# Stick-breaking attention of a two-block layer stack: its eight heads taken two at a time

## What is computed

```python
def stick_breaking(q, k, v):          # for each head and each block of 128 queries
    z = einsum("bhqd,bhkd->bhqk", qi, kh) * scale
    mask = kpos[None, :] < qpos[:, None]
    sp = where(mask, softplus(z), 0.0)
    rev = cumsum(sp, axis=3, reverse=True)
    w = exp(where(mask, z - rev, -inf))
    return einsum("bhqk,bhkd->bhqd", w, vh)
```

## Time and profile before

| what | us |
|---|---|
| median of three runs (lowest, highest) | 3726.54 (3718.42, 3730.17) |
| the profiled execution's own time | 3731.72 |
| its span, first to last instruction | 3729.7 |
| TensorE busy in it | 3562.5 (96%) |
| VectorE, ScalarE, GpSimd busy | 1577.5, 1385.2, 1464.3 |
| mean granted TensorE clock | 0.968 of full speed |

### The profile page before, as it was taken

The page is one execution under the profiler, slowest core; times in us unless marked ns, Lnnn a source line. Parts: engine busy times, 40 slices in busy tenths (PEclk is TensorE's granted clock), DMA queues, the critical chain, the costliest instruction groups (busy, mean ns, idle before and its releaser), DMA issues.

```text
span 3729.7 us, 39657 instructions
## 1 busy us (share of the span) xinstructions
PE 3562.5 (96%) x16304; PEld 2811.6 (75%) x16304; DVE 1577.5 (42%) x2130; ACT 1385.2 (37%) x2241; POOL 1464.3 (39%) x785
## 2 busy tenths in 40 slices
PE   7999999999999999999999999998989999989999
PEld 5887766777888788766787788775577787777887
DVE  4326563454432433755436343345535411443220
ACT  3444444223331444444323322254532323543221
POOL 2333333443554332333344455433034543224543
PEclk9999999999999999999999999988899999999999
DMA  6333211444553333311253555412025532212332
GB/s 208 106 103 114 62 46 51 124 141 124 166 171 109 103 113 101 110 51 44 72 144 113 152 164 151 126 54 62 0 65 162 164 94 87 70 53 85 96 96 74
DMA packets 566978, 385.30 MB, mean 103 GB/s; under 512 B 13598, under 2 KB 504302, under 8 KB 566798
## 3 DMA queue, kind: packets, MB, share of 16 engines
q1 hardware_dynamic: 564574, 379.56, 34.8%
q10 hardware_dynamic: 2224, 3.21, 0.3%
HBM read 379.25 MB, written 2.10 MB: 102 GB/s over the span
## 4 chain that ended last, share of the span: by engine, by line
PE 82%; DVE 7%; ACT 6%; POOL 3%; issue 1%; DMA 1%; SPq 0%; ACTq 0%; DVEq 0%; POOLq 0%
PE ps L174 81%; POOL wlo L144 2%; ACT whi L140 2%; ACT L136 1%; PE ps L178 1%; DVE H L152 1%; DVE mq L152 0%; ACT sxb L136 0%; DVE fg L152 0%; DVE ST L158 0%; DVE np L144 0%; DVE sp L152 0%; DMA W<-in_w_ada 0%; ACT xr L136 0%; ACT sp L136 0%
## 5 line engine op out<-in xcount | busy, mean ns | idle before, releaser
L144 POOL TENSOR_TENSOR wlo<-raw,whi 128x1024 fp32r<-128x1024 f32 (+1 forms) x540 | 1281.3, 2382 | 1944.4 <-ACT whi L140 1943.5
L174 PE MATMUL ps<-UH,whi 128*128 128x512 f32 x2656 | 1072.2, 404 | 26.8 <-ACT UH L140 16.2
L174 PE MATMUL ps<-UH,wlo 128*128 128x512 f32 x2656 | 1050.4, 395 | 26.2 <-POOL wlo L144 26.2
L174 PE MATMUL ps<-UL,whi 128*128 128x512 f32 x2656 | 1047.5, 394 | 0.0
L140 ACT ACTIVATE whi<-raw 128x1024 fp32r<-128x1024 f32 (+1 forms) x540 | 545.5, 1022 | 387.7 <-PE ps L174 193.5
L174 PEld LDWEIGHTS ps<-UH,whi 128*128 128x128 f32 x2656 | 507.0, 191 | 158.0 <-ACT UH L140 27.2
L174 PEld LDWEIGHTS ps<-UH,wlo 128*128 128x128 f32 x2656 | 507.3, 191 | 148.2 <-POOL wlo L144 38.3
L174 PEld LDWEIGHTS ps<-UL,whi 128*128 128x128 f32 x2656 | 506.1, 191 | 109.1 <-DVE UL L144 2.2
L152 DVE SCALAR_TENSOR_TENSOR ACC<-raw,SM,ACC 128x512 f32<-128x512 f32 x308 | 357.0, 1159 | 20.4 <-DVE GL L144 0.5
L174 PE MATMUL ps<-GH,whi 128*128 128x512 f32 x704 | 275.1, 391 | 0.0
L174 PE MATMUL ps<-GL,whi 128*128 128x512 f32 x704 | 274.0, 389 | 0.0
(11 more groups left out here) (335 smaller groups left out, 4260.7 us busy)
## 6 DMA issues: line engine op xcount, KB each, us to landing
raw<-in_w_in SPq DMA_DIRECT2D x168, 512.0 KB, 4.0
raw<-in_w SPq DMA_DIRECT2D x120, 512.0 KB, 5.1
raw<-in_ada_w SPq DMA_DIRECT2D x96, 512.0 KB, 4.8
raw<-in_w_ada SPq DMA_DIRECT2D x80, 512.0 KB, 4.8
raw<-in_ffn_w_gate SPq DMA_DIRECT2D x44, 512.0 KB, 3.9
raw<-in_ffn_w_up SPq DMA_DIRECT2D x44, 512.0 KB, 3.9
raw<-in_ffn_w_down SPq DMA_DIRECT2D x32, 512.0 KB, 4.0
raw<-in_ev_w_in SPq DMA_DIRECT2D x20, 512.0 KB, 3.8
```

What stands on the lines that cost most here:

```text
L144: return self.e.tensor_tensor(o, a, b, op).then_inc(*self.done(*keys))
L174: m = self.e.matmul(o, l, r, start=start, stop=stop)
```

## The change

Heads 2i and 2i + 1 are now handled as pair i on every engine. On TensorE the matmuls of the two alternate: in scores one reads rows 0 to 63 and the next rows 64 to 127, and in values one writes columns 0 to 63 of the array and the next columns 64 to 127. Scores of three pairs are issued before the first sums, and those of the fourth behind the sums of the first pair. Values of pair i stand behind the sums of pair i + 1, those of the last pair at the end. Score banks are 0 to 3 (were 0 to 2), sum banks 4 and 5 (were 3 to 5). There are eight `zs` tiles, the four new ones in the space of the normalised input, which has been consumed by then, and four `sp` tiles. ScalarE runs both Exp of a pair and then both Ln. The number of matmuls and their sizes stay the same, and so do VectorE's and GpSimd's.

```diff
-              zs=[at(f"zs{i}", (32, 37, 42, 72)[i], [128, 1280]) for i in range(4)],
-              sp=[at(f"sp{i}", 77 + 5 * i, [128, 1280]) for i in range(3)])
+              zs=[at(f"zs{i}", (32, 37, 42, 72)[i], [128, 1280]) for i in range(4)] +
+                 [at(f"zs{4 + i}", 68 + 5 * i, [128, 1280], F32, BASE) for i in range(4)],
+              sp=[at(f"sp{i}", 77 + 5 * i, [128, 1280]) for i in range(3)] + [at("sp3", 89, [128, 1280], F32, BASE)])
...
+                for x in range(2):
+                    h, r = 2 * i + x, slice(64 * x, 64 * x + 64)
+                    o = bank(p, (0, 1, 2, 3), ("z", h, kb), ("dve", ("z", h, kb)))
+                    p.mm(o[:, 0:n], EV["QK"][r, 4 + i, kb * 128:(kb + 1) * 128], EV["QK"][r, i, kb * 128:512],
+                         True, True, ("z", h, kb))
...
-                o = bank(p, (3, 4, 5), ("su", h, kb), ("dve", ("su", h, kb)))
+                o = bank(p, (4, 5), ("su", h, kb), ("dve", ("su", h, kb)))
...
+                for x in range(2):
+                    h = 2 * i + x
+                    p.wait_ge(*on("act", "ew", h, kb))
+                    p.mm(pv[64 * x:64 * x + 64, 128 * kb:512], EV["V"][:, kb, h * 64:(h + 1) * 64],
+                         EV["zs"][h][:, OFF[kb]:OFF[kb + 1]], kb == 0, kb == 3, *([("epv", i)] if kb + x == 4 else []))
+
+        scores(0)
+        scores(1)
+        scores(2)
+        for i in range(4):
+            later_keys(2 * i)
+            later_keys(2 * i + 1)
+            if i == 0:
+                scores(3)
+            else:
+                values(i - 1)
+        values(3)
...
+        for i in range(4):
+            weights(i)
+            if i < 2:
+                soft(i + 2)
+            if i:
+                out_tile(i - 1)
+        out_tile(3)
...
+        scores(0)
+        softs(0)
+        scores(1)
+        softs(1)
+        sums(0)
+        scores(2)
+        sums(1)
+        for i in range(4):
+            less(2 * i)
+            if i < 3:
+                sums(2 * i + 2)
+            less(2 * i + 1)
+            if i < 3:
+                sums(2 * i + 3)
+            if i == 0:
+                scores(3)
+            if i < 2:
+                softs(i + 2)
+            if i:
+                out_tile(i - 1)
+        out_tile(3)
```

More of the change, by code:

```diff
@@ L2255, in pe_even, with scores @@
                 lambda b: (v_lane(b), ("EV", b)), UH, UL, None, between)
-        def scores(h):
-            i, po = h // 2, 64 * (h % 2)
-            if h == 0:
+        def scores(i):
+            if i == 0:
                 for w in range(2):
@@ L2264, in scores, with later_keys @@
                 n = 512 - 128 * kb
[L2265 to L2273, removed]
+                for x in range(2):
[3 more added lines that the diff above has]
+                         True, True, ("z", h, kb))
+        def later_keys(h):
+            sp = EV["sp"][h % 4]
             p.wait_ge(*on("dve", "sp", h))
@@ L2280, in pe_even, with values @@
                          *([("su", h, kb)] if k2 == 3 else []))
-            if h < 6:
-                scores(h + 2)
-            if h == 0:
+        def values(i):
+            if i == 0:
                 for b in range(4):
                     p.wait_ge(*on(v_lane(b), "EV", b))
-            if h % 2 == 0:
-                pv = bank(p, (6, 7), ("epv", i), ("dve", ("eyl", 4 + i)))
+            pv = bank(p, (6, 7), ("epv", i), ("dve", ("eyl", 4 + i)))
             for kb in range(4):
-                p.wait_ge(*on("act", "ew", h, kb))
-                p.mm(pv[po:po + 64, 128 * kb:512], EV["V"][:, kb, h * 64:(h + 1) * 64], z[:, OFF[kb]:OFF[kb + 1]],
-                     kb == 0, kb == 3, *([("epv", h)] if kb == 3 else []))
+                for x in range(2):
[9 more added lines that the diff above has]
+            later_keys(2 * i + 1)
+            if i == 0:
+                scores(3)
+            else:
+                values(i - 1)
+        values(3)
     def xy(k):
@@ L2367, in act_even, with soft, weights, out_tile @@
         copy_ev(a)
[L2369 to L2374, removed]
+        def soft(i):
+            for x in range(2):
+                h = 2 * i + x
+                a.wait_ge(*on("dve", "ab", h))
+                a.af(EV["sp"][h % 4][:, :], EV["sp"][h % 4][:, :], ACT.Exp, ("ex", h))
+            for x in range(2):
+                h = 2 * i + x
+                a.wait_ge(*on("act", "ex", h))
+                a.af(EV["sp"][h % 4][:, :], EV["sp"][h % 4][:, :], ACT.Ln, ("ln", h), bias=1.0)
+        def weights(i):
+            for x in range(2):
+                h = 2 * i + x
+                for kb in range(4):
+                    z = EV["zs"][h][:, OFF[kb]:OFF[kb + 1]]
+                    a.wait_ge(*on("dve", "su", h, kb))
+                    a.af(z, z, ACT.Exp, ("ew", h, kb))
+        def out_tile(i):
+            a.wait_ge(*on("pe", "epv", i))
+            a.cp(EV["YH"][:, 4 + i, :], ps(("epv", i))[:, :], ("eyh", 4 + i))
         soft(0)
         soft(1)
[L2378 to L2388, removed]
+        for i in range(4):
[5 more added lines that the diff above has]
+        out_tile(3)
     def copy_ev(e):
@@ L2444, in dve_even, with scores, softs, sums @@
         copy_ev(v)
-        def scores(h):
-            z, sp = EV["zs"][h % 4], EV["sp"][h % 3]
+        def scores(i):
             for kb in range(4):
                 n = 512 - 128 * kb
-                if h > 3:
[L2451 to L2460, removed]
+                for x in range(2):
+                    h = 2 * i + x
+                    v.wait_ge(*on("pe", "z", h, kb))
+                    v.cp(EV["zs"][h][:, OFF[kb]:OFF[kb] + n], ps(("z", h, kb))[:, 0:n], ("z", h, kb))
+        def softs(i):
+            for x in range(2):
+                h = 2 * i + x
+                z = EV["zs"][h]
+                v.wait_ge(*on("pool", "zm", h))
+                if h > 3:
+                    v.wait_ge(*on("pe", "su", h - 4, 3))
+                v.stt(EV["sp"][h % 4][:, :], z[:, :], -1.0, z[:, :], ALU.mult, ALU.min, ("ab", h))
+        def sums(h):
+            z, sp = EV["zs"][h], EV["sp"][h % 4]
             v.wait_ge(*on("act", "ln", h))
             v.stt(sp[:, :], z[:, :], 0.0, sp[:, :], ALU.max, ALU.add, ("sp", h))
[L2464 to L2468, removed]
+        def less(h):
+            z = EV["zs"][h]
             for kb in range(4):
@@ L2473, in dve_even, with out_tile @@
                 v.tt(z[:, c], z[:, c], ps(("su", h, kb))[:, 0:n], ALU.subtract, ("su", h, kb))
[L2474 to L2482, removed]
+        def out_tile(i):
+            v.wait_ge(*on("act", "eyh", 4 + i))
+            v.tt(EV["YL"][:, 4 + i, :], ps(("epv", i))[:, :], EV["YH"][:, 4 + i, :].bitcast(F32), ALU.subtract, ("eyl", 4 + i))
+        scores(0)
[12 more added lines that the diff above has]
+                sums(2 * i + 3)
+            if i == 0:
+                scores(3)
[4 more added lines that the diff above has]
+        out_tile(3)
     def pool_even(g, after):
@@ L2493, in pool_even @@
             pool_split(g, soon("EV", "c", c))
-        for h in range(8):
+        for i in range(4):
             for kb in range(4):
-                dg = EV["zs"][h % 4][:, OFF[kb]:OFF[kb] + 128]
-                g.wait_ge(*on("dve", "z", h, kb))
-                g.asel(dg, ALU.is_gt, NEG, 1, *([("zm", h)] if kb == 3 else []))
+                for x in range(2):
+                    h = 2 * i + x
+                    g.wait_ge(*on("dve", "z", h, kb))
+                    g.asel(EV["zs"][h][:, OFF[kb]:OFF[kb] + 128], ALU.is_gt, NEG, 1, *([("zm", h)] if kb == 3 else []))
     OD = dict(YH=at("OYH", 0, [128, NT, S], F32R), YL=at("OYL", 16, [128, NT, S], F32R), QT=ring("oq", 32, 5, 512),
```

## The result

The changed kernel takes 3708.02 us, the median of five runs (3700.42 to 3712.01), against 3720.28 for the kernel before in five runs (3717.91 to 3730.17). The ratio is 0.9953, 95% interval 0.9937 to 0.9968: between 11.9 and 23.4 us less. The predicted time was 3708.2, in the range 3699 to 3720, and faster by over 0.3%.

The account below looks back on a forecast made before the run. No engine bounds the stage, a loop of dependences does: full-clock steps of 76.6 plus 4.0 for the clock make 80.6 against 98.9, 18.3 less; 3726.5 - 18.3 = 3708.2 us, range 3699 to 3720.

Parts of the forecast that it names:

- to the first sums: Stage start until TensorE's first sums, paced by VectorE's copies: 18.1 us at full clock, 10.5 before.
- sums of heads 0, 1: TensorE's sums of the first pair: 8.5 us, plus 0.4 for changes of kind and 0.6 of bank waits.
- scores of pair 3: TensorE's last scores, half finding free banks, half waiting for VectorE's `sp` of head 3 and four copies: 4.4 us.
- head 4's first banks and the wait: Head 4's sums fill both banks (3.5 us), then TensorE stands 5.95 while VectorE waits for ScalarE's output copy.
- rest of heads 4, 5: TensorE's remaining sums of heads 4 and 5 once VectorE goes on: 6.1 us.
- clock: Time added to the full-clock steps for half-clock stretches after TensorE idles: 4.0 us, between 0 and 11.5.
- The mechanism: In the stage: one long output stall, later first sums, paired matmuls at half cost, 9 table loads instead of 17.
- The rule that the prediction took over: From the Trainium skill: idle gaps between TensorE's bursts drop its clock; 1.60 us of idle preceded a 0.50 clock.
- Rival 1: Alternating halves of scores and values don't run side by side here: gain of only 8 us, 3718.5; chance 0.08.
- Rival 2: VectorE becomes the bound in the sums through two sum banks: 11.2 us more, gain 7.1, 3719.4; chance 0.09.
- Rival 3: TensorE stays at half clock through the whole stage: 12.2 us slower than before, 3738.7; chance 0.04.
- the wait for `YH`: VectorE's output 0 remainder waits for ScalarE's copy in head 4's sums, stalling TensorE 5.95 us, once instead of three times.

Follow-up runs that it names:

- the new order: Changed kernel with three sum banks, values of pairs 0 and 1 moved, ScalarE's output copies earlier and VectorE's list reordered: 3690.73 us, ratio 0.9924.

## Why the prediction was right

Point by point, in the order of its steps (predicted at full clock, measured):

| step | predicted | measured |
|---|---|---|
| to the first sums | 18.1 | 18.48 |
| sums of heads 0, 1 | 9.5 | 12.29 |
| scores of pair 3 | 4.4 | 4.39 |
| sums of heads 2, 3 | 10.5 | 10.62 |
| values of pair 0 | 2.3 | 2.30 |
| head 4's first banks and the wait | 9.5 | 9.31 |
| rest of heads 4, 5 | 6.1 | 7.81 |
| values of pair 1 | 2.3 | 2.31 |
| sums of heads 6, 7 | 9.5 | 9.68 |
| values of pairs 2, 3 | 4.4 | 4.46 |
| clock | 4.0 | in the rows above |
| stage | 80.6 | 81.65 |

- **The mechanism held**: one stall of 5.58 (5.95 predicted) in place of three waits of 4.40, sums later by 8.0 at the start (7.6), values of a pair side by side at half price, the table loads from 17 to 9. The two steps that the half clock stretched come out at full clock as well: sums of heads 0 and 1 take 9.68 where the idle was filled (9.5 predicted), and those of heads 4 and 5 take 9.68 where the output came later (3.5 + 6.1 predicted).
- **The clock** term was 4.0. The two steps that lie in half-clock stretches are 2.8 and 1.7 over their full-clock price, 4.5 in all; the third stretch, at 10.1 to 13.5, was hidden beside VectorE's copies, as argued. The 4.0 was picked between the ends 0 and 11.5 and not worked out, so that it lies within 0.5 is luck. Removing and filling idles showed that they have a part in the half clock. The rule that the prediction took over, that idle gaps drop the clock, isn't the whole of it: three gaps of 1.60 in the kernel before were followed by half clock, the one of 2.00 in the old kernel with its outputs later wasn't.
- **Rival 1** (halves not side by side) is out: records of a pair start within 0.02 us where nothing makes the second wait. Its price of 2.13 for values was about right: two heads cost 4.60 in the kernel before, 2.30 now. What was mis-sized is the expectation of the run with values apart, since heads listed one after the other in the changed kernel still overlap a little: 1.55 (and 1.25 for each of the last two) instead of 2.13. The last section shows it.
- **Rival 2** (VectorE as the bound through two sum banks): the banks cost 2.3 to 2.8 us net, not 11.2. That the halved scores bring nothing is nearly so: putting them apart again cost 1.75 at full clock, 5.15 in all.
- **Rival 3** (half clock throughout): half clock in 17.1 of 81.65 us.
- **What the prediction didn't see** is how much of the gain hangs on one instruction. I priced the wait for `YH` as 5.95 and went on; I didn't ask what it would cost to move it, which is 7.5 in the changed kernel and 10.8 in the old one. Through the clock a wait can cost more than its own length: in the old kernel 3.7 us of waiting had 7.1 of half clock with it.
- The difference was applied to a median of three, 3726.5. With five runs that median is 3720.28, so the measured difference of medians, 12.3, is less than the stage's 17.25, while the interval of the ratio (11.9 to 23.4 us) holds it. That the median hit to 0.2 us is luck: 18.3 was predicted, 12.3 measured, and the median subtracted from was 6 too high. That the stage hit to 1.05 is not, but for the clock's 4.0.

## What to carry to other kernels

Where no engine is the bound, step the new order with durations from rows, engine by engine, with every wait: it gave the ten steps of this stage to within 0.4 us, clock apart. Then look for the instruction that nobody needs soon (an output's copy) standing ahead of those that free a buffer, and try moving it first. Adding up saved work can fit the total and still name the wrong cause: 17.1 us of matmul time was to be saved, 17.25 were gained, but putting the halves apart again cost 5.75 at full clock, and one moved copy gave 7.5.

## What the runs showed of the hardware

Matmuls on the other half of the array can start ahead of some that stand before them in the list. With values apart, the second head's first matmul record began 1.56 us after the first head's first and 0.53 ahead of the latter's last record, while three records of the first head were still to start. So heads on opposite halves overlap a little even when listed one after the other, and a pair costs 3.85 us, where two heads in the kernel before cost twice 2.30.

Alternation gives half price only where nothing waits. Records of a pair of values start within 0.01 us of each other, and 16 of them take 2.30 us. The 16 score records of pair 3 have as many columns, but they take 4.39 in the change and 4.21 in the new order, nearly what they would take one behind the other (2560 columns, each twice, at 1.2 columns a ns: 4.27), since they wait for banks.
